# A two-layer diffusion block and a mixture of experts on one core: modulation work moved beside two scans, and more slabs as seven products

## What is computed

```python
for l in range(2):
    ml = silu(c) @ w_ada[l] + b_ada[l]        # 9 vectors of 1024, for the latent
    mc = silu(c_ctx) @ w_ada[l] + b_ada[l]    # the same 9 for the context
    lat = lat + 0.5 * ml[2] * swiglu(modulate(lat, g1, ml[0], ml[1]), w1, w3, w2)     # first feed-forward
    cx  = cx  + 0.5 * mc[2] * swiglu(modulate(cx,  g1, mc[0], mc[1]), w1, w3, w2)
    # token mixer: z = modulate(., gm, m[3], m[4]) @ w_in; a gated spatial product and
    # a two-way gated linear scan in 4 heads; times w_out and m[5]; the context first,
    # since its final states start the latent's scans
    # second feed-forward with m[6], m[7], m[8] (of the context in layer 0 only)
# swiglu(h) = (silu(h @ w1) * (h @ w3)) @ w2, with w1, w3 1024 x 2816 and w2 2816 x 1024
# modulate(x, g, shift, scale) = rmsnorm(x, g) * (1 + scale) + shift
```

## Time and profile before

| | us |
|---|---|
| median of 3 runs (3009.4 to 3009.75) | 3009.48 |
| the profiled execution | 3009.36 |
| its span | 3007.5 |
| TensorE busy | 2840.7 (94%) |
| VectorE busy | 1027.7 (34%) |
| ScalarE busy | 553.7 (18%) |
| GpSimd busy | 422.0 (14%) |

### The profile page before, as it was taken

The page is one execution under the profiler, slowest core; times in us unless marked ns, Lnnn a source line. Parts: engine busy times, 40 slices in busy tenths (PEclk is TensorE's granted clock), DMA queues, the critical chain, the costliest instruction groups (busy, mean ns, idle before and its releaser), DMA issues.

```text
span 3007.5 us, 39866 instructions
## 1 busy us (share of the span) xinstructions
PE 2840.7 (94%) x17362; PEld 2414.2 (80%) x17362; DVE 1027.7 (34%) x1988; ACT 553.7 (18%) x840; POOL 422.0 (14%) x424
## 2 busy tenths in 40 slices
PE   8999999999999999999999999999999999866766
PEld 6888888888888899899888888889988888533432
DVE  4864034431433334733014343423145312210111
ACT  2101222124111101010033116210012340200000
POOL 0000011100121075066001210038000000000000
PEclk9999999999999999999999999999999999888878
DMA  9765443344343556755444344364433228999998
GB/s 406 295 261 186 150 146 129 124 154 154 139 142 122 191 203 228 273 215 174 163 149 145 133 142 159 127 225 169 165 129 126 98 95 339 382 429 431 430 431 371
DMA packets 74146, 641.49 MB, mean 213 GB/s; under 512 B 8304, under 2 KB 9584, under 8 KB 17648
## 3 DMA queue, kind: packets, MB, share of 16 engines
q1 hardware_dynamic: 71376, 631.55, 55.3%
q10 hardware_dynamic: 2592, 7.33, 0.6%
HBM read 637.80 MB, written 1.05 MB: 212 GB/s over the span
## 4 chain that ended last, share of the span: by engine, by line
PE 86%; DMA 13%; DVE 1%; issue 0%; ACT 0%; POOL 0%; SPq 0%; DVEq 0%; POOLq 0%; ACTq 0%
PE ps L1364 30%; PE ps L1386 18%; PE ps L1340 12%; DMA ring<-in_w_moe 12%; PE ps L1561 7%; PE ps L1374 3%; PE ps L1397 3%; PE ps L1591 2%; PE ps L1145 2%; PE ps L1450 1%; DMA ring<-in_w_ada 1%; PE ps L1568 1%; PE ps L1167 1%; PE ps L1536 0%; PE ps L1539 0%; PE ps L1272 0%
## 5 line engine op out<-in xcount | busy, mean ns | idle before, releaser
L1364 PE MATMUL ps<-ring 128*128 128x256 f32 x2560 | 559.0, 379 | 0.1
L1364 PEld LDWEIGHTS ps<-ring 128*128 128x128 f32 x2560 | 484.0, 190 | 67.7 <-issue 1.9
L1386 PE MATMUL ps<-work,ring 128*128 128x256 f32 x2464 | 537.8, 379 | 0.0
L1386 PEld LDWEIGHTS ps<-work,ring 128*128 128x128 f32 x2464 | 466.1, 190 | 64.3 <-issue 2.1
L2029 DVE TENSOR_TENSOR work<-work,ps 128x128 f32<-128x128 f32 (+3 forms) x414 | 151.3, 400 | 610.9 <-PE ps L1364 286.5
L1364 PE MATMUL ps<-h,ring 128*128 128x256 f32 x1600 | 352.6, 381 | 6.4 <-ACT h L1784 4.2
L1364 PEld LDWEIGHTS ps<-h,ring 128*128 128x128 f32 x1600 | 302.2, 191 | 52.2 <-issue 5.6
L2760 POOL TENSOR_TENSOR ring<-ring 128x512 f32<-128x512 f32 x174 | 227.7, 1337 | 368.9 <-DMA ring<-in_w 315.7
L2788 POOL TENSOR_TENSOR work<-work 128x128 f32<-128x128 f32 x168 | 100.1, 633 | 1190.6 <-ACT work L1810 1190.6
L1340 PE MATMUL ps<-work,ring 128*128 128x128 f32 x1856 | 217.0, 275 | 0.3 <-POOL work L2760 0.3
L1340 PEld LDWEIGHTS ps<-work,ring 128*128 128x128 f32 x1856 | 212.0, 192 | 0.5 <-POOL work L2760 0.5
(11 more groups left out here) (300 smaller groups left out, 2591.4 us busy)
## 6 DMA issues: line engine op xcount, KB each, us to landing
ring<-in_w SPq DMA_DIRECT2D x210, 1024.0 KB, 4.9
work<-in_w_moe SPq DMA_DIRECT2D x22, 4096.0 KB, 33.8
ring<-in_w_moe SPq DMA_DIRECT2D x22, 4096.0 KB, 33.2
ring<-in_w_in SPq DMA_DIRECT2D x80, 1024.0 KB, 4.8
work<-in_w_ada SPq DMA_DIRECT2D x40, 1024.0 KB, 5.8
ring<-in_w_ada SPq DMA_DIRECT2D x32, 1024.0 KB, 4.8
ring<-in_w SPq DMA_DIRECT2D x28, 768.0 KB, 4.3
ring<-in_w_out SPq DMA_DIRECT2D x16, 1024.0 KB, 4.8
```

Of the source, the lines that this page charges most:

```text
L1364: last = nc.tensor.matmul(ps[:, b, c * L:c * L + L], w[:, k * L + c * P:k * L + c * P + P], hs[cols][:, k, :], start=(k == 0), stop=(k == ...
L1386: last = nc.tensor.matmul(ps[:, b, c * L:c * L + L], w[:, k * L + c * P:k * L + c * P + P], hid[:, k0 + k, :], start=(k0 + k == 0 and c == 0),
```

## The change

- `HALVED` gets the pairs 6 to 10 of (0,1,0); `HALVED_DOWN` gets (0,1,0), (0,0,1), (1,0,0) and (1,0,1).
- Of the ten vectors that VectorE takes, seven were in (0,1,0) and three in down of (0,0,1). Now three (layer 0, vectors 2 to 4) are in (0,1,0), spread over its first 14 slabs instead of all 34; three (5 to 7) beside the first scan, four (vector 8 and 0 to 2 of layer 1) beside the second. The `ada` slabs behind the second scan's projection now make vectors 3 and 4 of layer 1 instead of 0 and 1.
- Pieces are loaded one by one (512 KB) by ScalarE: `prime` loads the first four (two in the scans), and each `vada` stage on ScalarE waits until VectorE is done with that piece and loads the piece that takes its buffer. The buffers lie at `uv_at` and `ex_at` (in the scans only at `uv_at`, so two). Beside the scans there is a single accumulator, so a vector's first piece waits for the `vsum` of the one before.
- `vsum` and `turn` use the four turning PSUM groups instead of banks of their own. `halves` of (0,1,0) comes behind the last piece, since it uses the same space.

```diff
-HALVED = {(0, 0, 1): range(1, 11), (1, 0, 0): range(1, 11), (1, 0, 1): range(2, 11)}
+HALVED = {(0, 1, 0): range(6, 11), (0, 0, 1): range(1, 11), (1, 0, 0): range(1, 11), (1, 0, 1): range(2, 11)}
-HALVED_DOWN = []
+HALVED_DOWN = [(0, 1, 0), (0, 0, 1), (1, 0, 0), (1, 0, 1)]
+A_GAPS = 14
+def one_by_one(vectors):
+    out, turns = [], []
+    for l, i in vectors:
+        out += [[("vada", l, 4 * i + part, c)] for part in range(4) for c in range(2)] + [[], [("vsum", l, i)]]
+        turns.append((len(out) + 1, ("turn", l, i)))
+    out += [[], []]
+    for at, turn in turns:
+        out[at].append(turn)
+    return out
+def beside(scan, pieces, first, phase):
+    out = [list(bundle) for bundle in scan]
+    out[first - 1].append(("prime", phase))
+    for i, bundle in enumerate(pieces):
+        out[first + i * (len(out) - first) // len(pieces)] += bundle
+    return out
...
-            read = [n for n in range(slabs[mine[0]]) if plan[n][0] == "gmlp"]
+            read = [n for n in range(slabs[mine[0]]) if plan[n][0] in ("gmlp", "vada")]
...
     run = (0, 1, 0)
-    side = vector_ada(0, 2, 9)
+    side = vector_ada(0, 2, 5)
+    side[0].insert(0, ("prime", 0))
...
-    plan += spread_out(gate_up(run, range(11)) + down(run, range(4)), side)
+    plan += spread_out(gate_up(run, range(11)) + down(run, range(4)), side, A_GAPS)
...
     side = [[("gmlp", 0, 1), ("decay", 0, 1, 0)]] + heads(0, 1) + [[("osquare", 0, 1)], [("osum", 0, 1)]]
+    side = beside(side, one_by_one([(0, 5), (0, 6), (0, 7)]), 2, 1)
...
     side = [[("gmlp", 0, 0), ("decay", 0, 0, 0)]] + heads(0, 0) + [[("osquare", 0, 0)], [("osum", 0, 0)]]
+    side = beside(side, one_by_one([(0, 8), (1, 0), (1, 1), (1, 2)]), 2, 2)
...
-    plan += spread_out(gate_up(run, range(11)), side) + spread_out(down(run, range(4)), vector_ada(1, 2, 5))
+    plan += spread_out(gate_up(run, range(11)), side) + down(run, range(4))
...
(SyncE)
-                    if stage[0] == "vada" and stage[3] == 0:
-                        ...
-                        sp.dma_start(ada_w[k % len(ada_w)], a["w_ada"][l * 4 * N_MOD + i]).then_inc(a_full[k % len(ada_w)], 16)
(ScalarE)
+                    elif kind == "prime":
+                        if stage[1]:
+                            act.wait_ge(gm_out, stage[1])
+                        for piece in at.primed[stage[1]]:
+                            load_piece(piece)
+                    elif kind == "vada":
+                        k = at.ada_piece[stage[1:]][0]
+                        if k in at.ada_next:
+                            act.wait_ge(a_free, k + 1)
+                            load_piece(at.ada_next[k])
(VectorE)
-                        if part == c == 0 and nth >= 2:
+                        if part == c == 0 and at.phase_of[l, i]:
+                            dve.wait_ge(acc_sum, nth)
+                        elif part == c == 0 and nth >= 2:
                             dve.wait_ge(acc_sum, nth - 1)
```

More of the change, by code:

```diff
@@ L392, in __init__ @@
                 self.slabs += 1
-            if kind in ("gate", "up", "z", "wo", "mem", "msum", "xsum", "sum", "hsum", "in2", "proj", "out2") or (kind == "down" and stage[5] == 0):
+            if kind in ("gate", "up", "z", "wo", "mem", "msum", "xsum", "sum", "hsum", "in2", "proj", "out2") or (kind == "down" and stage[5] == 0) or kind == "vsum":
                 assert groups < 4 or self.freed[groups - 4], (n, stage)
@@ L522, in __init__ @@
                 self.summed[stage[1:]] = len(self.summed)
+                open_at[stage[1:]] = self.group[n]
             elif kind == "turn":
@@ L525, in __init__ @@
                 self.turn_at[stage[1:]] = self.d
+                if stage[1:] in self.summed:
+                    self.group[n] = open_at[stage[1:]]
+                    self.freed[self.group[n]] = ("d", self.d)
             elif kind == "square":
@@ L611, in build @@
         ckt = shaped(pmt[:, 10 * P:14 * P], 2, 2, P)
-        adac = shaped(pmt[:, 0:8 * P], 2, 2, L)
         gm = shaped(glamask[:, 0:8 * P], 8, P)
@@ L860, in build, with acc_of @@
         assert lf_at + 2 * KF * P <= uv_at
+        def acc_of(vector):
+            return 1 if at.phase_of[vector] else at.summed[vector] % 2
         def ring_place(k):
@@ L1280, in first @@
                     elif kind == "vsum":
-                        vector = stage[1] * N_MOD + stage[2]
-                        pe.wait_ge(a_free, 4 * at.summed[stage[1:]] + 4)
-                        pe.wait_ge(ev_d, at.turn_at[divmod(vector - 2, N_MOD)])
+                        b = fresh()
+                        pe.wait_ge(a_free, 8 * at.summed[stage[1:]] + 8)
                         for r in range(2):
                             for q in range(4):
-                                last = nc.tensor.matmul(ps[32 * q:32 * q + 32, 4 + vector % 2, r * L:r * L + L], ones[:, 0:32],
-                                                        acc[at.summed[stage[1:]] % 2][:, r, q * L:q * L + L],
+                                last = nc.tensor.matmul(ps[32 * q:32 * q + 32, b, r * L:r * L + L], ones[:, 0:32],
+                                                        acc[acc_of(stage[1:])][:, r, q * L:q * L + L],
                                                         start=(r == 0), stop=(r == 1), skip_group_check=True)
@@ L1296, in first @@
                                     o = 8 * c + 4 * r
-                                    last = nc.tensor.matmul(ps[:, 6 + vector % 2, o:o + 4], adac[:, vector % 2, r, c * P:c * P + P],
+                                    last = nc.tensor.matmul(ps[:, at.group[n] % 4, o:o + 4], adac[:, vector % 2, r, c * P:c * P + P],
                                                             v("turn", 0, 8).rearrange("p (q r) -> p q r", r=2)[:, :, 0],
@@ L1676, in own, with load_piece @@
                 act.wait_ge(act_own, S.next(act_own))
+            def load_piece(piece):
+                l, i, c = piece
+                buffer = at.ada_piece[piece][1]
+                act.dma_start(ada_w[buffer], a["w_ada"][l * 4 * N_MOD + i, :, c * 4 * L:c * 4 * L + 4 * L]).then_inc(a_full[buffer], 16)
             def first():
```

64 lines of the change are left out of this document (34 added, 30 removed).

## The result

The changed kernel takes 3047.16 us (median of 4 runs, 3045.19 to 3047.81), the kernel before 3009.61 us beside it: a ratio of 1.0121, 95% interval 1.0106 to 1.0137. It is slower, as forecast, but by 37.6 us where I had 10; 3047 lies outside my range. The profiled execution took 3047.45 us, with a span of 3045.6.

A forecast was written before the change was run, and what follows sets the result against it. TensorE was taken as the bound (86% of the chain of waits), VectorE taking over in the first feed-forward. Terms 11+22.6-10.9-7.1-5.5=+10.1 us on 3009.36 us gave 3019.5 us, +0.33%, range 2996 to 3034 us.

The forecast's parts named there:

- S: Time in the first feed-forward when the first w_ada piece lands for VectorE: 59 us, bounds 43 and 62.
- Halved down sets: Down sets in seven products: each falls from 75.97 to 68.8 us, saving 7.1 us; four sets give 28.5 us.
- rival 4: Halved down slabs stay near 6.9 us because GpSimd falls behind, losing up to 28 us of saving: 3045 us; 4%.
- Rival 1: First feed-forward not bound by VectorE, as the first pieces land early (S=45): 2992.5 us; 20%.
- the prediction's two terms: Scans: a piece ahead of a decay delays it 2.5 us; one beside the keys delays them another 2.5.
- Stage A: The context's first feed-forward, 31.25 to 275.17 us before; forecast to end at 286 us, +11 us (bounds -9 to +17).
- Together 88 us: First feed-forward: VectorE's work from S until the sums of h are done, ahead of slab 13, ending at 147 us.
- the lock: VectorE and GpSimd exclude each other for whole two-operand SBUF instructions; 6 us taken in the first feed-forward, 0 to 10.
- 133 us to the end: First feed-forward after the sums of h: slab rest 4.5, nine halved slabs 56.3, vsum and turn 2.5, down 68.8, clock 1.
- 12.6 us of `vsum` and `turn`: Certain cost on TensorE of seven vectors moved to the two scans, 3 to the first and 4 to the second.
- Stalls: 10 us: Both scans: waits from pieces ahead of decays and beside GpSimd's keys, 0 to 20 us; 2 us in the second.
- Rival 3: Pieces of heads 2 and 3 lock the scans' keys, 7 to 8 us per head: 30 us instead of 10, 3038 us; 13%.

The follow-up runs named there:

- experiment 8: Kernel before with only the down sets of (1,0,0) and (1,0,1) in seven products, no piece moved: 2997.58 us (0.9959).
- Experiment 1: Changed kernel with ScalarE issuing the first four w_ada pieces ahead of the ten constants instead of behind them: 3046.13 us (1.011).
- experiment 4: Changed kernel with VectorE's operations on pieces beside the scans cut to 128 of 1,024 columns: 3979.6 us, experts getting other tokens; only the scans compared.
- experiments 6 and 11: Changed kernel, two variants: scan pieces placed with the empty and score bundles, 3051.19 us (1.0137); each scan turn one bundle later, 3051.29 us (1.0141).
- experiment 9: Changed kernel with the first feed-forward's gate and up slabs in eight products, its down set in seven, pieces over 24 gaps instead of 14: 3007.51 us (0.9994).
- experiment 3: Changed kernel with the first feed-forward's last ten gate and up slabs in eight products again, its down set still in seven: 3035.44 us (1.0082).

## Why the prediction was wrong

**Right.** The direction. S: 59.95 against 59 us. Halved down sets: 68.8 us, as worked out, so that rival 4 is out, though its 3045 us lie nearest to the measured time; that is chance. From the down set of (0,0,1) to the next gate slab 79.0 us (1249.87 to 1328.90), as worked out. (1,0,0) and (1,0,1): -12.0 against -12.6, and -12.2 in experiment 8. Rival 1 is out by S. Experiment 1 is no test of it, since there the constants still stand ahead of the fifth piece; it shows that the prediction's rule "each us that S is smaller gives back one" doesn't hold where only the first four pieces come sooner.

**Luck.** The waits at the scores of the first scan: about 2 and 5 us forecast, 2.37 and 5.31 measured. But the keys of heads 2 and 3 end 9.8 and 9.2 us later than before, measured from the scores of the head before, where the prediction's two terms make 5 a head.

**Stage A, 12 us too little.** The step that failed is "Together 88 us". From the first piece to the end of the sums of h VectorE took 103 us (59.95 to 162.95); with the lock I had 94. The terms: the sums of hid that the halved down set adds ahead of the sums of h, 6 us, which I had counted for GpSimd's cover and not here; the lock, 3.4 us on hid and 3.9 on pieces, 7.3 instead of 6; a wait of 2.2 us for an `up` that TensorE's own waits had made late; S, 1 us. That is 153+6+1.3+2.2+1=163.5. Behind it I had 133 us to the end and it took 135.2; the slow slab at 163.01 alone is 2.7. I allowed 1 us for the clock.

The clock itself was seen as forecast, only more often: in the stretches around the first wait (length, busy times, clock, DMA share, GB/s) the granted clock is 0.50, 1.2 GHz, while TensorE has nothing to do and into the work that follows, and 1.00 (2.4 GHz) ahead of it.

```profile
70.00:75.00 5.00, 3.21 (x15) 2.47 (x14) 3.88 (x5) 1.42 (x3) 0.00 (x0) 1.00 0.90 338
...
80.00:85.00 5.00, 0.00 (x0) 0.00 (x0) 4.86 (x9) 0.00 (x0) 0.00 (x0) 0.50 0.33 115
85.00:90.00 5.00, 2.48 (x18) 1.20 (x19) 4.83 (x8) 1.88 (x2) 0.00 (x0) 0.50 0.66 187
```

Ahead of 163 us these slow slabs cost little of their own, since VectorE sets the end there, with one exception: the slab at 144.60 takes 8.83 us instead of 7.07, and VectorE waits 2.18 us for its result.

**The scans, 10 us too little.** 12.6 us of `vsum` and `turn` stand. The step that failed is "Stalls: 10 us": 20.3 were measured, 11.4 in the first scan, where I had 8, and 8.9 in the second, where I put 2 us and looked only at the scores. There the wait was at the `vsum` (VectorE's last piece just too late) and at the `turn` (ScalarE's copy): 5.0 us, and 1.8 of slow clock. In the first scan the waits at the scores are 7.7 us, and 2.8 us of slow matmuls followed them, for which the scans had no term. Together the scans give 12.6+7.7+2.8+5.0+1.8=29.9 of 32.9 us. The remaining 3 us are open; experiment 4 has them too, in its second scan, so they aren't VectorE's time on the pieces. Three placings of the pieces (changed, experiments 6 and 11) give scans of 486, 491 and 488 us against 453 before: in each of the three a vector costs 4.7 us or more, not 1.8. Rival 3 had the lock alone at 30 us of stalls; the keys of the heads take 0.9 to 5.9 us longer, not 7 to 8. (Its own terms give 3039.5 us, not 3038, and those of rival 4 3047.5, not 3045.)

**(0,0,1), 5.6 us too little saved.** All of it lies ahead of its down set: the prediction's sum begins at the down set and put nothing on the start of the run. The gate slab of its start waits for weights, 4.35 us, where it had waited 1.27; every kernel here that has pieces beside the second scan shows such a wait or one for ScalarE, 2.1 to 4.4 us, and the two without them show 1.3. Why the load is late was not tried. The rest, 2.4 us, is slow clock in the two slabs behind this wait. In experiment 9 that wait is 2.31 us and the stage is 8.7 us shorter than before.

**What the whole was.** The 14 gaps and the ten halved slabs made stage A lose: without both it is 13 us shorter than before (experiment 9), with both 23 longer. Without the halved slabs alone it is 12 longer (experiment 3). The other way round, these slabs with more gaps, was not tried: their sums of h use the space of the pieces, so the pieces have to be done ahead of them. The move costs 26 us and makes room for two halved down sets, of 7.1 us each at best. The two sets that need no room pay, 12 us. Whether the other two could be halved with the vectors left where they were was not tried.

## To carry to other kernels

Work handed to VectorE must be costed as one sum over the stretch in which it is due, with every helper operation in it, and with what GpSimd's operations beside it add: 24 pieces due in 14 slabs cost 25 us more than the same 24 due in 24. Moving work beside a stage with idle engines isn't free if that stage has a chain through several engines: look at the slack of each link (here 6.5 and 1.7 us), and at both ends of what is moved, its last producer and its copy. Take the part of a change that needs nothing moved first; here it was the only part that made the kernel faster.

## What was not expected of the hardware

VectorE's multiplication by a scalar with one SBUF operand and GpSimd's key products delay each other too: eight of 0.75 us take 6.98, beside keys that take 12.42 instead of 8.3 us. The Trainium skill ("SBUF — State Buffer", Who interferes with whom) has this, where I had looked at two operands only: a tensor_scalar can run in a mode that takes the second port pair too, and is then locked out by GpSimd and locks it out. The trace agrees: 1,024 columns in 0.75 us, where the two-operand form takes 1.25.

And a wait of 1.03 us at 872.75 was followed by a clock of 0.88 and 0.69, while those of 1.62 us at 932.82 and of 1.03 at 990.56 were followed by 1.00. What makes the difference no run here shows:

```profile
872.00:876.00 4.00, 3.25 (x17) 2.91 (x18) 4.00 (x4) 0.70 (x3) 4.00 (x5) 0.88 0.80 261
876.00:880.00 4.00, 4.00 (x15) 3.29 (x14) 2.78 (x5) 1.28 (x1) 4.00 (x6) 0.69 0.29 56
...
932.00:936.00 4.00, 3.18 (x19) 2.93 (x20) 3.62 (x3) 2.64 (x5) 4.00 (x5) 1.00 0.81 258
```
